# First attention: copies ahead of maxima on VectorE, and softmax sums taken by ScalarE in place of products with ones

## The reference

```python
def _attend(q, k, v):                    # per block of 128 queries
    s = jnp.einsum('bqkgd,bskd->bkgqs', qblk, kf) * scale
    p = jax.nn.softmax(s, axis=-1)
    return jnp.einsum('bkgqs,bskd->bqkgd', p, vf)
...
# prompt: 128 queries, keys are the prompt's own 128
# latent: 256 queries, keys are 128 cached ones and the latent's own 256
y = jnp.concatenate([y_hy, o.reshape(b, n, GQA_Q)], axis=-1) @ ev_w_out[i]
```

## Time and profile before

| | |
|---|---|
| Time, median of 3 runs | 1063.71 us (1060.15 to 1063.98) |
| Profiled execution, its own time | 1053.43 us |
| Its span | 1051.6 us |
| Mean granted clock of TensorE | 0.902 |
| TensorE (PE) busy | 871.4 us |
| VectorE (DVE) busy | 405.0 us |
| ScalarE (ACT) busy | 266.0 us |
| First attention, from the first scores to the first output product | 269.8 to 327.1 us |

### The profile page before, as it was taken

One profiled execution on the slowest core, in us unless ns is written; L12 is line 12 of the kernel. 1 busy time (PEld: TensorE's weight loads), 2 busy tenths in 40 slices (PEclk: granted clock), 3 DMA queues, 4 the chain that ended last, 5 costly groups with the idle time before them and its releaser, 6 DMA issues.

```text
span 1051.6 us, 12188 instructions
## 1 busy us (share of the span) xinstructions
PE 871.4 (83%) x4438; PEld 507.5 (48%) x4438; DVE 405.0 (39%) x851; ACT 266.0 (25%) x597; POOL 92.8 (9%) x120
## 2 busy tenths in 40 slices
PE   2898999999868988997766788788789998998760
PEld 0346765536423555554323446656566455554320
DVE  1467273551253342321106264563833332422114
ACT  1134011201320332221113335343332232222111
POOL 1000000000000012000021030312300012000002
PEclk9998999999688988999985899888869987999995
DMA  8980264246900188999999672020105188999975
GB/s 236 381 275 1 80 171 144 80 160 165 355 0 1 46 332 299 397 411 411 393 380 398 240 283 100 1 81 1 40 1 185 60 304 316 389 412 411 408 281 189
DMA packets 86417, 231.79 MB, mean 220 GB/s; under 512 B 8832, under 2 KB 18561, under 8 KB 86041
## 3 DMA queue, kind: packets, MB, share of 16 engines
q1 hardware_dynamic: 72418, 193.88, 50.0%
q0 software_dynamic: 7616, 26.95, 7.3%
q10 hardware_dynamic: 6328, 10.22, 2.7%
HBM read 216.40 MB, written 17.52 MB: 222 GB/s over the span
## 4 chain that ended last, share of the span: by engine, by line
PE 60%; DMA 16%; DVE 9%; issue 5%; ACT 5%; DVEq 3%; ACTq 1%; SPq 1%; POOLq 0%; POOL 0%
PE ps L836 54%; DMA ring<-in_moe_w_up_dram 7%; DMA ring<-in_w_mod_dram 5%; PE ps L843 4%; DVEq L1792 3%; DMA arena<-in_moe_w_up_dram 2%; ACT arena L1490 2%; ACTq L636 1%; PE ps L1038 1%; DMA arena<-in_moe_w_down_dram 1%; SPq L653 1%; ACT hT L1521 1%; DMA hT<-h_rows,rows_in 1%; DVE negmax L1860 1%; DVE statA L1916 1%
## 5 line engine op out<-in xcount | busy, mean ns | idle before, releaser
L836 PE MATMUL ps<-arena 128*64 128x256 f32 (+12 forms) x1332 | 290.0, 444 | 41.7 <-DVE arena L1855 11.1
L836 PEld LDWEIGHTS ps<-arena 128*64 128x64 f32 (+4 forms) x1332 | 171.2, 188 | 143.7 <-issue 69.3
L836 PE MATMUL ps<-ring,hT 128*128 128x512 f32 (+2 forms) x384 | 133.9, 508 | 7.7 <-ACT hT L1521 3.5
L836 PE MATMUL ps<-ring,arena 128*64 128x256 f32 (+1 forms) x864 | 124.8, 432 | 16.3 <-DMA ring<-in_moe_w_down_dram 8.4
L836 PEld LDWEIGHTS ps<-ring,hT 128*128 128x128 f32 x384 | 73.0, 192 | 65.0 <-issue 60.6
L836 PEld LDWEIGHTS ps<-ring,arena 128*64 128x64 f32 x864 | 60.7, 136 | 65.9 <-issue 39.9
L836 PE MATMUL ps<-ring,condT 128*32 128x512 f32 x384 | 62.0, 762 | 25.0 <-DMA ring<-in_w_mod_dram 19.0
L843 PE MATMUL ps<-ident,arena 128*128 128x128 f32 (+2 forms) x276 | 51.9, 317 | 35.7 <-ACT arena L1541 10.8
L1490 ACT ACTIVATE arena<-ps 128x256 f32<-128x256 f32 (+4 forms) x91 | 41.8, 495 | 123.1 <-PE ps L836 112.5
L2117 DVE TENSOR_TENSOR arena<-arena,ps 128x128 f32<-128x128 f32 x37 | 10.7, 288 | 138.8 <-ACT arena L1568 138.8
L836 PE MATMUL ps<-hT,ring 128*128 128x384 f32 x192 | 62.1, 486 | 0.0
(11 more groups left out here) (284 smaller groups left out, 920.9 us busy)
## 6 DMA issues: line engine op xcount, KB each, us to landing
ring<-in_w_mod_dram SPq DMA_DIRECT2D x48, 1024.0 KB, 10.0
ring<-in_moe_w_down_dram SPq DMA_DIRECT2D x24, 1024.0 KB, 17.8
ring<-in_moe_w_gate_dram SPq DMA_DIRECT2D x42, 512.0 KB, 14.2
ring<-in_moe_w_up_dram SPq DMA_DIRECT2D x42, 512.0 KB, 16.4
arena<-in_moe_w_gate_dram SPq DMA_DIRECT2D x32, 512.0 KB, 8.0
arena<-in_moe_w_up_dram SPq DMA_DIRECT2D x32, 512.0 KB, 9.8
arena<-in_moe_w_down_dram SPq DMA_DIRECT2D x13, 1024.0 KB, 13.3
ring<-in_ev_w_in_dram SPq DMA_DIRECT2D x9, 1024.0 KB, 12.6
```

The lines of the kernel that those rows point to most:

```text
L836: mm = pe.matmul(out, lhsT, rhs, **kw)
```

## The change

VectorE's loop does `pair_copy(i - 2)` before `pair_max(i)`, and ScalarE's does `second_copy(i - 2)` before `pair_probs(i)`.

The sums come from ScalarE: every exponential of this attention also accumulates its row sum into `psumexp` (24 columns, one per unit). `tile_sums(t)`, at `i` 5, 9 and 13 on VectorE, takes the reciprocals of the tile's 8 columns, 128x8, into `rinv`. They have the queries on the partitions, while the join needs them along the columns, so three small steps turn and spread them. TensorE transposes `rinv` to 8x128 (`sums_turn`, ahead of the values); VectorE multiplies it by a mask (`own_column`) into `masked`, 8 rows by 4 x 128 columns, where row `h` keeps only the block of its own head (`tile_mask`); and TensorE multiplies by `half_rows`, 8 rows by 128, which sends rows 0 to 3 to the first 64 partitions and rows 4 to 7 to the others (`sums_spread`, after the values). Both results go through bank 7, so the spread waits for the mask. ScalarE copies the spread result to `reci`, behind the exponentials of pair 7 or 11 or after the loop, and `tile_join` waits for that copy. The products with ones and the 128x512 reciprocal are gone. The two masks come with the constants, whose table grows from 42 to 48 columns; `half_rows` is made by a copy where `onesv` was set.

```diff
@@ -86,7 +86,7 @@
-VALUES_AT, JOIN_AT = {6: 0, 10: 1}, {7: 0, 11: 1}
+SUMS_AT, VALUES_AT, JOIN_AT = {5: 0, 9: 1, 13: 2}, {6: 0, 10: 1}, {7: 0, 11: 1}
@@ -106,7 +106,9 @@
-    c["tables"] = np.tile(np.concatenate([below, i - 3, i - 2, 2 * (e // 2), [0, HALF]]), (P, 1))
+    r = np.arange(P)[:, None]
+    c["tables"] = np.concatenate([np.tile(np.concatenate([below, i - 3, i - 2, 2 * (e // 2), [0, HALF]]), (P, 1)),
+                                  r % 4 == i, r // 4 == np.arange(2)], 1)
@@ -257,7 +259,7 @@
-    B.stage("gL", NT, (7,))
+    B.stage("gL", 2 * NT, (7,))
@@ -385,7 +387,7 @@
-        tables = sb("tables", P, 42)
+        tables = sb("tables", P, 48)
@@ -397,7 +399,7 @@
-        psumexp = sb("psumexp", P, len(units_mla))
+        psumexp = sb("psumexp", P, 2 * NPAIRS)
@@ -438,6 +440,7 @@
+        own_column, own_half = tables[0:QH, 42:46], tables[0:QH, 46:48]
@@ -472,7 +475,8 @@
-        onesv = ropeq[:, 0, 0, :]
+        half_rows = filtc[0:QH, 3:3 + P]
+        masked = modrow[0:QH, :]
@@ -541,6 +545,7 @@
+        sums_ready = sem("sums_ready")
@@ -1008,21 +1013,22 @@
             def tile_values(t):
                 for u in (QH * t + QH - 2, QH * t + QH - 1):
                     drained_wait(pe, "gPT", u)
-                total, bank = claim("gL", t), claim("gO", t)
+                bank = claim("gO", t)
                 v0 = (QH + KVH) * HD
-                for name, out in (("gL", total), ("gO", bank)):
-                    for s in range(1 if t == 0 else NT):
-                        for g in range(KVH):
-                            if name == "gL":
-                                lhs = onesv
-                            elif t and s == 0:
-                                lhs = cv[:, g * HD:(g + 1) * HD]
-                            else:
-                                lhs = qkv[:, s, v0 + g * HD:v0 + (g + 1) * HD]
-                            pT = turned_probs[t]
-                            rhs = pT[:, 2 * g:2 * g + 2, :, :] if t == 0 else pT[:, s, 4 * g:4 * g + 4, :]
-                            mm = product(out[HD * g:HD * g + HD, :], lhs, rhs, start=s == 0, stop=t == 0 or s == NT - 1)
-                    fill_inc(mm, name, t)
+                for s in range(1 if t == 0 else NT):
+                    for g in range(KVH):
+                        lhs = cv[:, g * HD:(g + 1) * HD] if t and s == 0 else qkv[:, s, v0 + g * HD:v0 + (g + 1) * HD]
+                        pT = turned_probs[t]
+                        rhs = pT[:, 2 * g:2 * g + 2, :, :] if t == 0 else pT[:, s, 4 * g:4 * g + 4, :]
+                        mm = product(bank[HD * g:HD * g + HD, :], lhs, rhs, start=s == 0, stop=t == 0 or s == NT - 1)
+                fill_inc(mm, "gO", t)
+
+            def sums_turn(t):
+                pe.wait_ge(sums_ready, t + 1)
+                fill_inc(turn(claim("gL", 2 * t)[0:QH, 0:P], rinv[:, 0:QH]), "gL", 2 * t)
+
+            def sums_spread(t):
+                fill_inc(product(claim("gL", 2 * t + 1)[:, :], half_rows, masked, start=True, stop=True), "gL", 2 * t + 1)

             def experts(l):
                 for b, n in enumerate(B.jobs[f"moe{l}"]):
@@ -1360,8 +1366,12 @@
                 if i < NPAIRS:
                     pair_scores(i)
                 if i in VALUES_AT:
+                    sums_turn(VALUES_AT[i])
                     tile_values(VALUES_AT[i])
+                    sums_spread(VALUES_AT[i])
+            sums_turn(NT - 1)
             tile_values(NT - 1)
+            sums_spread(NT - 1)
             for c in range(NCH):
                 drained_wait(pe, "inv1", c)
             moe(0)
@@ -1553,7 +1563,7 @@
-                    drain_inc(act.activation(probs[:, i % 2, r, 0:nk], bank_of("gS", u)[:, 0:nk], ACT.Exp, bias=negmax[:, u:u + 1]), "gS", u)
+                    drain_inc(act.activation(probs[:, i % 2, r, 0:nk], bank_of("gS", u)[:, 0:nk], ACT.Exp, bias=negmax[:, u:u + 1], accum_out=psumexp[:, u:u + 1]), "gS", u)
@@ -1722,10 +1732,13 @@
             for i in (5, 6):
                 mod_step("gqa", i)
             for i in range(NPAIRS + 2):
+                if i >= 2 and i % 2:
+                    second_copy(i - 2)
                 if i < NPAIRS:
                     pair_probs(i)
-                if i >= 2 and i % 2:
-                    second_copy(i - 2)
+                if i in JOIN_AT:
+                    copy_out("gL", 2 * JOIN_AT[i] + 1, reci, bank_of("gL", 2 * JOIN_AT[i] + 1)[:, :])
+            copy_out("gL", 2 * NT - 1, reci, bank_of("gL", 2 * NT - 1)[:, :])
             moe(0)

             act.activation(statA[:, 1, 0:1], statA[:, 0, 0:1], ACT.Sqrt)
@@ -1885,11 +1898,20 @@
                     bank = filled_wait(dve, "gPT", 2 * i + r)
                     drain_inc(dve.tensor_copy(*turned_copy(i, r, bank[:, 0:nk])), "gPT", 2 * i + r)

+            def tile_sums(t):
+                for u in (QH * t + QH - 2, QH * t + QH - 1):
+                    drained_wait(dve, "gS", u)
+                dve.reciprocal(rinv[:, 0:QH], psumexp[:, QH * t:QH * t + QH]).then_inc(sums_ready, 1)
+
+            def tile_mask(t):
+                bank = filled_wait(dve, "gL", 2 * t)
+                shape = [QH, 4, P]
+                drain_inc(dve.tensor_tensor(masked.rearrange("p (a b) -> p a b", b=P), bank[0:QH, 0:P].unsqueeze(1).broadcast_to(shape),
+                                            own_column.unsqueeze(2).broadcast_to(shape), ALU.mult), "gL", 2 * t)
+
             def tile_join(t):
-                bank = filled_wait(dve, "gL", t)
-                drain_inc(dve.reciprocal(reci, bank[:, :]), "gL", t)
-                settle()
                 bank = filled_wait(dve, "gO", t)
+                drained_wait(dve, "gL", 2 * t + 1)
                 by_tok = lambda a: a.rearrange("p (a b) -> p a b", b=P)
                 drain_inc(dve.tensor_tensor(hT[:, 4:8, t * P:(t + 1) * P], by_tok(bank[:, :]), by_tok(reci), ALU.mult), "gO", t)

@@ -2299,7 +2321,7 @@
-                    ins = dve.memset(onesv, 1.0)
+                    ins = dve.tensor_copy(half_rows.rearrange("p (g d) -> p g d", d=HD), own_half.unsqueeze(2).broadcast_to([QH, KVH, HD]))
@@ -2340,12 +2362,17 @@
             for i in range(7):
                 mod_step("gqa", i)
             for i in range(NPAIRS + 2):
+                if i >= 2:
+                    pair_copy(i - 2)
+                if i in SUMS_AT:
+                    tile_sums(SUMS_AT[i])
                 if i < NPAIRS:
                     pair_max(i)
-                if i >= 2:
-                    pair_copy(i - 2)
+                if i in VALUES_AT:
+                    tile_mask(VALUES_AT[i])
                 if i in JOIN_AT:
                     tile_join(JOIN_AT[i])
+            tile_mask(NT - 1)
             tile_join(NT - 1)
             moe(0)

```

## The result

The changed kernel takes 1046.41 us (median of 4 runs, 1041.73 to 1049.35) where the kernel before took 1061.93 (4 runs beside it, 1060.13 to 1063.98). The ratio is 0.985 with a 95% interval of 0.980 to 0.990: 15.5 us less, against the 18 that were forecast. The profiled execution took 1041.73 us with a span of 1039.9.

A forecast was written before the change was run, and what follows sets the result against it. The first attention was taken as bound by a chain turning from engine to engine, none full. 8.2 - 3.2 + 9.1 + 7.0 = 21.1 us, less 3 for clock falls: 1063.7 - 18 = 1045.7 us; range 1040 to 1058.

The forecast's parts named there:

- The ring and the places of the idles: First attention: copies waiting behind maxima and joins leave TensorE idle; new layout has 8.3 us idle, was 17.4, saving 9.1.
- Sums off TensorE: First attention: the products with ones leave TensorE's path, 8.2 us saved.
- What was put in: TensorE in the first attention: three small transpositions, 0.6 us, and three spread products, 2.6 us; 3.2 us added.
- The reads: ScalarE, after each exponential: a 0.193 us read of the accumulated sum; taken as costing nothing, 0.8 us at its high bound.
- The clock: TensorE in the first attention: 2.4 GHz from about 276 us, 7.0 saved, less 3 for falls after two idles.
- the forecast's band: Whole kernel: 14 to 23 us saved, chance 0.66.
- rival 1: First attention: TensorE's clock stays low, so only 4 to 14 us are saved; chance 0.22.
- The rule of the Trainium skill: Small idles between matmul groups swing TensorE's clock; without any clock gain, 14 us or less saved instead of 18.
- Transfers took nothing back: Rival on the weight stream behind the first attention: paced by time, not TensorE, so nothing saved, 1063.7; chance 0.05.
- The output products began at the high clock: Rival of a slower kernel: output products start and stay at low clock, ending over 0.5% slower; chance 0.04.
- the fourth rival: Joins of the first attention: nothing idles there, ScalarE's copy comes early, 23 us or more saved; chance 0.03.

The follow-up runs named there:

- order_only: Kernel before with only the new orders on VectorE and ScalarE, products with ones and the large reciprocal kept: 1050.63 us, ratio 0.9905, window 47.1 us.
- old_order_scalar: Changed kernel with joins one step later, but ScalarE's exponentials again ahead of its second copy: window 44.6 us, one execution.
- filler_slow: sums_only plus unused products with ones on TensorE ahead of the values, which overwrite them: 1052.57 us, window 56.2 us, one execution.
- reads_only: Kernel before with ScalarE's accumulated sums switched on and used by nobody: window 56.2 us against 57.3, one execution.
- the second comparison: The changed kernel measured once more, unedited, beside later experiments, against the kernel before: 1049.56 us, ratio 0.9863, window 41.2 us.
- sums_only: Changed kernel with both old orders put back on VectorE and ScalarE, sums from ScalarE kept: 1054.93 us, ratio 0.9964, window 54.6 us.

## Why the prediction was right, and which terms were off

- **The ring and the places of the idles: right.** The starts laid out for the transpositions of pairs 0 to 3 were 271.6, 273.0, 274.4 and 276.5; they came at 271.76, 273.22, 274.56 and 276.76. Pairs 7 and 11 were to have idles of 2.2 and 3.1; they had 2.00 and 2.85. In all I gave 8.3 of idle and 9.1 saved; it was 6.7 and 10.7. That it was the order is shown by order_only (10.2 us in the window for it alone, 9.6 in the medians), and by old_order_scalar that VectorE's half brings little without ScalarE's. Of ScalarE's half the prediction gave no price.
- **Sums off TensorE: 8.2 us is what their records held, and the window doesn't give it back in full.** Alone the sums brought 2.7 us in the one window and 5.3 in the medians. In that window the clock was lower, and filler_slow gives the work back for 1.6 us. At the high clock the work was worth some 6.2 us; the rest of the 8.2 was the low clock, and belongs with the term of the clock.
- **What was put in: 3.9 instead of 3.2.** Each spread took 1.05 us from its start to the next one's, at the high clock (283.44 to 284.49), where I took the 0.87 of a product over 128 rows. The mask took 0.67, close to the 0.69 that I took.
- **The reads: nothing to speak of, as taken** (reads_only). On ScalarE they do cost: two exponentials of 384 columns start 0.57 us apart with them and 0.48 without.
- **The clock: the term that was mis-sized.** I gave 7.0 for an early rise less 3 for falls, 4.0 net. What was left after the other terms is 16.3 - 8.2 + 3.9 - 10.7 = 1.3. The rise, laid at 276, came at about 281.2: the granted clock was 0.50 in 276:280 and 0.84 in 280:284, though TensorE had no idle from 271.76 on. These 5.2 us more at half speed are some 2.6 us of work (an estimate). The step that failed is how the rise was read off the kernel before. I put it at 287.5, but the rows give 0.50 up to 288 and 0.91 in 288:292, so it was at about 288.7, 5.5 us after the idle that ended at 283.26. Even with that it would have come at 277; it came 9.5 us after 271.76. The other part is the idle of 2.0: charged with half a fall, it cost a whole one (0.63 in 292:296), in both profiles of the kernel. The two low stretches of the first, about 291.5 to 294.9 and 305.2 to 308.6, are some 1.7 us each, 3.4 where I charged 3. 7.0 - 2.6 - 3.4 = 1.0 is near the 1.3 that was left.
- **The sum:** 18 forecast, 16.3 in the window, 15.5 in the medians; 1045.7 and 1046.4 us. The two lie closer than the terms deserve, and part of that is luck. The median of before was 1.8 us lower in this comparison than in the runs shown. Two errors, 1.6 too little for the idle and 2.7 too much for the clock, worked against each other. And in the second comparison the change saved 10.5 us, which is less than the 14 with which the forecast's band began, and inside the band of rival 1, though its window was 41.2 again.
- **The rivals.** That the clock stays low was the one that took its share, though far from the end at which only 4 us are saved. The rule of the Trainium skill (TensorE: Matmul & The Clock Gate, section "A second HAM failure mode: psum-queue depth-cycling") by which small idles between groups of matmuls let the clock swing, is borne out in part: the changed kernel had two falls and a mean of 0.79, and sums_only 0.66, but filler_slow kept its clock through three gaps of 1.57. The 16.3 us lie between the 14 or less that went with the rule and the 18. Transfers took nothing back: SP's send moved by 16.2 us. The output products began at the high clock (27.73 us for 64 records, 0.43 each). The joins did idle, so the fourth rival didn't come true either.

In the first profile the span is shorter by 11.7 us only, where the output products start 16.1 earlier. It was not lost right behind the stretch: SP's sends are 16.2 us ahead at 346.58 and 18.7 ahead at 465.96, then 14.4 at 785.87. Outside the stretch TensorE has the same work, 4276 records against 4277, and is busy 841.1 us with it where it was 831.5; the mean clock of the whole span is 0.898 where it was 0.902. So some of that work ran at a lower clock. Why is open: nothing there was changed, and the second profile, with nearly the same window, has a span of 1051.2 against 1039.9.

## What to carry to other kernels

When two engines pass work round in a ring, go through each engine's own order of calls and ask for every wait whether something already possible stands behind it. Here two such swaps, one on each of two engines, were worth 10 us together, and leaving out the second cost 10 us of a stretch of 34. Taking work off an engine can be worth less than its time, when its clock falls in the gaps that are left, as in the window of sums_only: cost it with these gaps, and take them out in the same change. And a whole time that moves by some us from one comparison to the next, as here 15.5 and 10.5 for one kernel, doesn't tell which term was right; the window does. A step that only collects a result, as the join does, belongs one step behind the point where it is ready: moving it took two lines and brought another 6.5 us of this stretch.

## What was not expected of the hardware

- In the changed kernel TensorE had no idle from 271.76 on, and the clock rose 9.5 us later, at 281.2. In the second profile of the same kernel it rose 7.0 us after the last idle (275.92 to about 283.0), and in the kernel before 5.5 us after the idle that ended at 283.26. What makes the difference is open.
- An idle of 2.0 us was followed by a fall in both profiles of the change, while three gaps of 1.57 in a row at the high clock in filler_slow (ahead of the transpositions at 291.87, 295.56 and 298.99) were not. In sums_only the clock fell at about 293.6, when the last gap had been one of 0.84. So the length of the last idle alone doesn't tell whether a fall follows.
- The float32 product over 8 rows took 1.05 us to the next start, where one over 128 rows in a row of its kind took 0.87, both at the high clock. Whether the 8 rows do it, or its place as a single product between others, no run tells. Its records:

```profile
L841 PE MATMUL ps<-modrow,filtc x6: 587/640/692, 283.4 to 310.4; 8*128 8x512 f32 x6
```
